# Gate and up products of a split-float32 feed-forward block: high and low x side by side in one 512-column matmul

## The reference

```python
def _rms_norm(x, g):
    y = x * lax.rsqrt(jnp.mean(x * x, axis=-1, keepdims=True) + NORM_EPS)
    return y * g

def _swiglu(x, w_gu, w_down):                  # d_ff 2816, eight times
    g, u = jnp.split(x @ w_gu, 2, axis=-1)
    return (jax.nn.silu(g) * u) @ w_down

def conv_ffn(x, w_up, conv_w, conv_b, w_down): # d_ff 3072, twice
    h = causal_depthwise_conv(x @ w_up, conv_w, conv_b)      # 3 taps along the tokens
    return (jax.nn.gelu(h[..., :D_FF_2]) * h[..., D_FF_2:]) @ w_down
```

## Time and profile before

| | us |
|---|---|
| median of 3 runs | 3186.62 |
| lowest, highest | 3185.95, 3188.76 |
| profiled execution, its own time | 3187.94 |
| its span in the trace | 3186.1 |
| PE busy | 2922.5 (92%) |
| DVE busy | 2079.8 (65%) |
| ACT busy | 1435.7 (45%) |
| mean granted TensorE clock, share of full speed | 0.957 |

### The profile page before, as it was taken

One profiled execution on the slowest core, in us unless ns is written; L12 is line 12 of the kernel. 1 busy time (PEld: TensorE's weight loads), 2 busy tenths in 40 slices (PEclk: granted clock), 3 DMA queues, 4 the chain that ended last, 5 costly groups with the idle time before them and its releaser, 6 DMA issues.

```text
span 3186.1 us, 46638 instructions
## 1 busy us (share of the span) xinstructions
PE 2922.5 (92%) x19567; PEld 2661.9 (84%) x19567; DVE 2079.8 (65%) x2681; ACT 1435.7 (45%) x1867; POOL 309.2 (10%) x391
## 2 busy tenths in 40 slices
PE   7997779999988999999799999877899889987898
PEld 7997769999975999995389999877899779885897
DVE  5668776565657656552665565787765767746776
ACT  4445435444444544442554444444444534444453
POOL 0005430000002000000000000345100000000000
PEclk9998889999999999999999999988999889997899
DMA  7553225676541665642146565432465446542553
GB/s 231 184 158 111 93 79 186 186 206 189 159 139 47 192 188 182 182 134 84 60 139 186 159 210 184 135 93 80 132 186 172 161 144 197 174 146 73 165 177 102
DMA packets 404053, 478.25 MB, mean 150 GB/s; under 512 B 16394, under 2 KB 331492, under 8 KB 403844
## 3 DMA queue, kind: packets, MB, share of 16 engines
q1 hardware_dynamic: 400432, 467.33, 47.0%
q0 software_dynamic: 1776, 6.77, 0.7%
q10 hardware_dynamic: 1636, 1.18, 0.1%
HBM read 474.17 MB, written 1.05 MB: 149 GB/s over the span
## 4 chain that ended last, share of the span: by engine, by line
PE 81%; DVE 14%; ACT 3%; issue 2%; ACTq 0%; DVEq 0%
PE Wk L570 15%; PE Wk L572 15%; PE Wk L571 15%; PE Y L570 9%; PE Y L571 9%; PE Y L572 9%; DVE w_lo L1511 3%; DVE work L1739 2%; PE Wk L578 2%; DVE work L1742 1%; PE Y L896 1%; PE Y L676 1%; PE Wk L869 1%; PE Y L804 1%; ACT w_hi L1103 1%
## 5 line engine op out<-in xcount | busy, mean ns | idle before, releaser
L1511 DVE TENSOR_TENSOR w_lo<-ring,w_hi 128x1024 fp32r<-128x1024 f32 x872 | 1061.0, 1242 | 628.8 <-ACT w_hi L1103 582.5
L570 PE MATMUL Wk<-xT_hi,w_hi 128*128 128x256 f32 x4320 | 1234.2, 286 | 19.3 <-DVE xT_lo L1543 15.9
L572 PE MATMUL Wk<-xT_hi,w_lo 128*128 128x256 f32 x4320 | 1227.9, 284 | 0.0
L571 PE MATMUL Wk<-xT_lo,w_hi 128*128 128x256 f32 x4320 | 1227.8, 284 | 0.0
L1103 ACT ACTIVATE w_hi<-ring 128x1024 fp32r<-128x1024 f32 x872 | 893.7, 1053 | 640.4 <-PE Wk L572 432.1
L570 PEld LDWEIGHTS Wk<-xT_hi,w_hi 128*128 128x128 f32 x4320 | 834.4, 193 | 27.0 <-issue 13.4
L571 PEld LDWEIGHTS Wk<-xT_lo,w_hi 128*128 128x128 f32 x4320 | 834.4, 193 | 4.7 <-issue 0.9
L572 PEld LDWEIGHTS Wk<-xT_hi,w_lo 128*128 128x128 f32 x4320 | 833.8, 193 | 0.0
L570 PE MATMUL Y<-w_hi,hid_hi 128*128 128x512 f32 x896 | 351.9, 393 | 4.3 <-DVE hid_lo L1597 4.3
L571 PE MATMUL Y<-w_lo,hid_hi 128*128 128x512 f32 x896 | 350.6, 391 | 0.0
L572 PE MATMUL Y<-w_hi,hid_lo 128*128 128x512 f32 x896 | 349.4, 390 | 0.0
(11 more groups left out here) (247 smaller groups left out, 3039.9 us busy)
## 6 DMA issues: line engine op xcount, KB each, us to landing
ring<-in_ffn_w_gu SPq DMA_DIRECT2D x352, 512.0 KB, 4.5
ring<-in_ffn_w_down SPq DMA_DIRECT2D x224, 512.0 KB, 4.4
ring<-in_ffn_w_up SPq DMA_DIRECT2D x96, 512.0 KB, 6.0
ring<-in_hg_w_in SPq DMA_DIRECT2D x80, 512.0 KB, 4.2
ring<-in_na_w_in SPq DMA_DIRECT2D x24, 512.0 KB, 4.5
ring<-in_hg_w_out SPq DMA_DIRECT2D x16, 512.0 KB, 4.1
ring<-in_lru_w_in SPq DMA_DIRECT2D x16, 512.0 KB, 4.5
ring<-in_kv_w SPq DMA_DIRECT2D x16, 512.0 KB, 4.9
```

Source lines behind the costliest of these rows:

```text
L570: pe.matmul(o, l_hi, r_hi, start=first, stop=False)
L571: pe.matmul(o, l_hi, r_lo, start=False, stop=False)
L572: return pe.matmul(o, l_lo, r_hi, start=False, stop=last)
L1511: dve.tensor_tensor(lo, raw(u), hi.bitcast(F32), ALU.subtract).then_inc(lo_done, 1)
```

## The change

The high and low parts of x lie side by side, `xT[:, k, 0, :]` and `xT[:, k, 1, :]`. For a block of weights, one matmul with the high weights runs over both (512 columns) and puts w_hi x_hi in the left half of a bank and w_hi x_lo in the right half; a second one with the low weights adds w_lo x_hi to the right half. So result and correction come apart, a product takes two banks (one for each f) and not one, and gate and up take all four banks of `Wk`: there is one set per chunk where there were two. ACT copies the right halves out (`save_rest`), DVE adds the left ones. PE waits before each gate product for the read of the last gate (`gate_read`, in cffn `conv_raw`), before each up product for that of the last up (`up_read`). In cffn ACT makes the tap with the bias. The products of the other sublayers keep their three matmuls.

```diff
-        xT_hi, xT_lo = sb("xT_hi", [P, KD, T], F32R), sb("xT_lo", [P, KD, T], F32R)
+        xT = sb("xT", [P, KD, 2, T], F32R)
+        xT_hi, xT_lo = xT[:, :, 0, :], xT[:, :, 1, :]
...
+        def with_rest(b):
+            return bank(b, 2).rearrange("p (f c t) -> p f c t", f=2, c=2)
...
+            def f_wide(u, b, f):
+                (t, h), (hi, lo) = u, split_of(u)
+                for i in range(4):
+                    k, c, o = 4 * h + i, 256 * i + P * f, bank(b + f)
+                    pe.matmul(o, hi[:, c:c + P], xT[:, k, :, :].rearrange("p c t -> p (c t)"), start=k == 0, stop=False)
+                    mm = pe.matmul(o[:, T:2 * T], lo[:, c:c + P], xT_hi[:, k, :], start=False, stop=k == KD - 1)
+                return mm
...
-                def gate_up(t, h):
-                    f_product(t, bank(2 * h))
-                    f_product(t + 1, bank(2 * h + 1))
+                def gate_up(j):
+                    if by_tokens(s):
+                        pe.wait_ge(conv_raw, 2 * (c0 + j) - 1)
+                    else:
+                        pe.wait_ge(gate_read, f0 + j)
+                    f_product(t0 + 3 * j - 1, 0, f_wide)
+                    if by_tokens(s):
+                        pe.wait_ge(conv_raw, 2 * (c0 + j))
+                    else:
+                        pe.wait_ge(up_read, f0 + j)
+                    f_product(t0 + 3 * j, 2, f_wide)
...
-                enter(s, (bank(0), bank(1)))
+                enter(s, (0, 2), f_wide)
...
                     if s == 0 and j == 1:
+                        pe.wait_ge(gate_read, 2)
                         first_parameters()
...
+            def save_rest(t, b, o):
+                act.wait_ge(unit_done, units_to(t))
+                act.activation(o, with_rest(b)[:, :, 1, :], ACT.Copy).then_inc(rest_saved, 1)
...
                     splits(g + 3)
+                    save_rest(g + 1, 0, gate_rest[:, j % 2])
                     if j == 0 and has_norm(s):
                         save_r(s)
                     splits(g + 4)
                     gate(j, j % 2, g)
+                    if j >= 2:
+                        act.wait_ge(hidden_ready, n0 + j - 1)
+                    save_rest(g + 2, 2, up_rest[:, j % 2])
                     rest(j, j % 2, g)
...
+                def last_tap(j, h, g):
+                    for gu in range(2):
+                        act.wait_ge(conv_raw, 2 * (c0 + j) + gu + 1)
+                        for f in range(2):
+                            act.activation(cf_out[:, h, gu, f, :], cf_raw[:, h, gu, f, 2:2 + T], ACT.Identity,
+                                           scale=..., bias=...).then_inc(conv_tap, 1)
...
                     dve.wait_ge(unit_done, units_to(g + 1))
-                    dve.tensor_tensor(wide(ff_silu[:, h, :]), wide(bank(2 * h)), r_wide(2), ALU.mult)\
+                    gate, up = with_rest(0), with_rest(2)
+                    dve.wait_ge(rest_saved, 2 * (n0 + j) + 1)
+                    dve.tensor_tensor(wide(ff_silu[:, h, :]), gate[:, :, 0, :], wide(ff_silu[:, h, :]), ALU.add)\
+                        .then_inc(gate_read, 1)
+                    dve.wait_ge(gate_read, f0 + j + 1)
+                    dve.tensor_tensor(wide(ff_silu[:, h, :]), wide(ff_silu[:, h, :]), r_wide(2), ALU.mult)\
                         .then_inc(gate_scaled, 1)
...
                     dve.wait_ge(unit_done, units_to(g + 2))
-                    hidden_parts(j, h, n0, ff_silu[:, h, :], bank(2 * h + 1))
+                    dve.wait_ge(rest_saved, 2 * (n0 + j) + 2)
+                    dve.tensor_tensor(wide(ff_hid[:, h, :]), up[:, :, 0, :], wide(ff_hid[:, h, :]), ALU.add)\
+                        .then_inc(up_read, 1)
+                    dve.wait_ge(up_read, f0 + j + 1)
+                    hidden_parts(j, h, n0, ff_silu[:, h, :], ff_hid[:, h, :])
...
-                    splits(g + 4)
-                    dve.wait_ge(conv_raw, 2 * (c0 + j + 1))
-                    for n, (gu, f) in enumerate(four):
-                        step(dve.tensor_scalar(cf_out[:, h, gu, f, :], cf_raw[:, h, gu, f, 2:2 + T], w(2, gu, f),
-                                               b(gu, f), ALU.mult, ALU.add), wait=n == 3)
+                    for gu in range(2):
+                        splits(g + 3 + gu)
+                        dve.wait_ge(unit_done, units_to(g + 1 + gu))
+                        dve.wait_ge(rest_saved, 2 * (n0 + j) + gu + 1)
+                        raw_ = cf_raw[:, h, gu, :, 2:2 + T]
+                        dve.tensor_tensor(raw_, with_rest(2 * gu)[:, :, 0, :], raw_, ALU.add).then_inc(conv_raw, 1)
+                    dve.wait_ge(conv_tap, 4 * (c0 + j + 1))
```

More of the change, by code:

```diff
@@ L208, in build @@
         y_part = sem("y_part")
+        gate_read, up_read, rest_saved = sem("gate_read"), sem("up_read"), sem("rest_saved")
         gate_scaled, z_read, c_mean, p_mean = sem("gate_scaled"), sem("z_read"), sem("c_mean"), sem("p_mean")
@@ L594, in f_product @@
                     for f in range(2):
-                        mm = f_part((t, h), o, f)
+                        mm = part((t, h), o, f)
                     mm.then_inc(unit_done, 1)
@@ L677, in turn, with enter @@
                 mm.then_inc(xT_psum, 1)
-            def enter(s, o):
+            def enter(s, o, part=f_part):
                 t = base[s]
@@ L685, in enter @@
                     pe.wait_ge(xT_ready, 4 * (s + 1))
-                    f_product(t, o[0])
-                    f_product(t + 1, o[1])
+                    f_product(t, o[0], part)
+                    f_product(t + 1, o[1], part)
                     return
@@ L704, in enter @@
                 for f in range(2):
-                    mm = f_part((t, 1), o[0], f)
+                    mm = part((t, 1), o[0], f)
                 mm.then_inc(unit_done, 1)
@@ L716, in enter @@
                 for f in range(2):
-                    mm = f_part((t + 1, 1), o[1], f)
+                    mm = part((t + 1, 1), o[1], f)
                 mm.then_inc(unit_done, 1)
@@ L1144, in save_r, with ffn_stages @@
                 act.activation(r_row[:, :], bank(6)[:, 0:T], ACT.Copy).then_inc(r_ready, 1)
-            def ffn_stages(s, chunks, gate, rest):
-                t0 = base[s]
+            def save_rest(t, b, o):
+                act.wait_ge(unit_done, units_to(t))
+                act.activation(o, with_rest(b)[:, :, 1, :], ACT.Copy).then_inc(rest_saved, 1)
+            def ffn_stages(s, chunks, gate_rest, up_rest, gate, rest):
+                t0, n0 = base[s], before(s, {"ffn": FF_CHUNKS, "cffn": CF_CHUNKS})
                 for j in range(chunks):
@@ L1193, in rest @@
                     hidden_hi(j, h, n0)
-                ffn_stages(s, CF_CHUNKS, both, rest)
+                ffn_stages(s, CF_CHUNKS, *(cf_raw[:, :, gu, :, 2:2 + T] for gu in range(2)), lambda j, h, g: None,
+                           last_tap)
             def sigmoid(z, done):
@@ L1492, in _ @@
                     act.preload_act_table_set("natural_log_exp_and_others")
-                if kind == "hg":
-                    hgrn(s, idx)
+                if kind in ("hg", "cffn"):
+                    {"hg": hgrn, "cffn": cffn}[kind](s, idx)
                 else:
-                    {"ffn": ffn, "cffn": cffn, "na": na, "mla": mla, "lru": lru, "stick": stick}[kind](s)
+                    {"ffn": ffn, "na": na, "mla": mla, "lru": lru, "stick": stick}[kind](s)
                 splits(end[s] + 1)
@@ L1610, in ffn @@
                     dve.wait_ge(unit_done, units_to(g + 1))
-                    dve.tensor_tensor(wide(ff_silu[:, h, :]), wide(bank(2 * h)), r_wide(2), ALU.mult)\
+                    gate, up = with_rest(0), with_rest(2)
[4 more added lines that the diff above has]
+                    dve.tensor_tensor(wide(ff_silu[:, h, :]), wide(ff_silu[:, h, :]), r_wide(2), ALU.mult)\
                         .then_inc(gate_scaled, 1)
+                    if s == 0 and j == 1:
+                        save_parameters(range(1, 7), 0)
                     splits(g + 4)
```

33 lines of the change are left out of this document (12 added, 21 removed).

## The result

The changed kernel takes 3212.4 us (median of 4 runs, 3210.6 to 3215.3), the kernel before, measured beside it, 3186.3 us (4 runs, 3185.8 to 3188.8). The ratio is 1.008, interval 1.0068 to 1.0093: 26 us or 0.8% **slower**. That is 21 us above the predicted time and at the upper edge of the range (3212), within rival (c)'s 3205 to 3214. Its profiled execution spans 3211.2 us, against 3186.1.

The account below looks back on a forecast made before the run. The prediction took TensorE (PE), busy 92% of the span, as the bound. Its terms, -42 + 25.6 + 8 + 0.7 + 12 = +4 us, gave about 3191 us beside the median of 3186.6, range 3174 to 3212.

Parts of the forecast that it names:

- rival (c): Slower: alternating widths cost wide matmuls their full 0.232 to 0.235 us, narrow ones no quicker; 3205 to 3214 us, chance 0.18.
- part 1: Gate and up products: three 256-column matmuls per weight block become one of 512 and one of 256, -42 us.
- chunk 1's gate waits: At each ffn's start PE waits for DVE's gate add, queued behind four w_lo: 8 x 3.2 = +25.6 us.
- ffn's end: In the last chunk an extra ACT copy and DVE add delay hid_lo, so PE waits: 8 x 1.0 = +8 us.
- cffn: The add and ACT's two up taps replace four DVE taps, about 0.3 us longer: +0.7 us for both sublayers.
- clock: Most of PE's eight waits at ffn starts are followed by a short stretch at clock 0.50: 8 x 1.5 = +12 us.
- all but the matmuls: The waits at ffn starts and ends, the cffn and the clock: 25.6 + 8 + 0.7 + 12 = 46.3 us.
- a sign of being wrong: For the alternating matmuls: the forecast is wrong if a pair takes over 0.352 or under 0.344 us.
- Rival (b): Faster: clock mostly stays up after the ffn-start waits and the matmul gain is at its upper end; 3174 to 3179, chance 0.16.
- Rival (d): The 13 ns belong to the columns, not the matmul, so a pair still costs 359.7 ns; 3233 us, chance 0.03.
- Rival (e): The eight ffn-start waits don't appear because DVE's four w_lo run ahead of r_row; 3154 us, chance 0.05.
- edit at nothing: At an ffn's start, chunk 1's up product comes 5.6 us behind its gate, so up_read is there first: no cost.

Follow-up runs that it names:

- e3: The changed kernel with each 512-column matmul made as two of 256 again, new banks and waits kept: 3234.6 us, ratio 1.0151.
- e5: The changed kernel, but at an ffn's start DVE makes the four w_lo, then adds the gate, and only then waits for r_row: 3173.5 us, ratio 0.9956.
- e6: On top of e5, each ffn's last up product made by three matmuls into one bank, without copy or add: 3164.7 us, ratio 0.9931.
- e4: The changed kernel, but at an ffn's start DVE adds the gate before making the four w_lo and waiting for r_row: 3190.8 us, ratio 1.001.
- e7: On top of e6, 200 of 224 products run all sixteen 512-column matmuls first, then all sixteen 256-column ones: 3148.0 us, ratio 0.9876.
- e1: The changed kernel with matmuls grouped, four of 512 columns and then four of 256: 3207.4 us, ratio 1.0064.
- e2: The changed kernel, but the narrow matmul adds to the left half of the bank instead of the right: 3211.8 us in one run.

## Why the prediction was right in its waits and wrong in its matmuls

| step | predicted | measured | from |
|---|---|---|---|
| matmuls (part 1) | -42 us, 348 ns a pair | -21 to -22 us, 352.8 ns | timeline; e3 |
| chunk 1's gate waits | 8 x 3.2 us | 8 x 3.2 us | timeline; e5 |
| ffn's end | 8 x 1.0 us | 7 x 1.06 and 1.34 us | timeline; e6 |
| cffn | +0.7 us | +1.1 us | timeline |
| clock | 8 x 1.5 us | 12.1 us; 7 of 8 fall | timeline, windows; e4 and e5 leave 9 and 13 |
| all but the matmuls | +46.3 us | +47.4 us | e3 |
| sum | +4 us | +26 us | runs |

**What failed is one term, the size of the gain in part 1.** It took 348 ns for a pair, "the value nearest to the alternating pattern", from two rows: one wide matmul behind a narrow one (0.24) and one narrow behind a wide one (0.11), together 0.35. Three things were wrong with that. First, each of those two is only the first matmul of a long run, and their sum 0.35 was already over the 348 that I took; I let the value slip towards that of undisturbed runs. Second, the rows show five disturbed wide matmuls in a row (0.232 on average), so that at a change in every matmul none would be free of it; I used that only for the far end of the range. Third, I gave each narrow one the full 0.11, and in the alternating stream only one in three is that quick. With 352.8 the pair fell even a little outside the bounds that I gave it (28 to 46.6 us; it is 24.9), and over the 0.352 us that I had named as a sign of being wrong. The down product's slower start, 4 us, I had not counted at all. So 17 of the 21 us are the pair and 4 the down product.

**Rival (c) is what happened**, by its own point of decision: a pair over 350 ns. Its rows spoke plainly for it, and 0.18 was too low a chance. Its picture was not exact either: the narrow one is somewhat quicker (116.5) and the wide one dearer (236.3) than it said. Rival (b) needed the clock to stay up behind more than five waits, and it did behind one. Rival (d) is out by e7: 359.7 - 347.1 = 12.6 ns go with every matmul that is saved, as long as widths aren't mixed. That is five times what the Trainium skill's 2.5 ns ("TensorE: Matmul & The Clock Gate", "Back-to-back issue gap") would give, a figure that the section states for a matmul by itself and not for a stream with weight loads. Rival (e) is out by the timeline.

**The waits were right** to a tenth of a microsecond, but for one, because they were read from the queue of the engine that must free the banks, not from its busy share. **The clock's total was right partly by luck**: eight falls of 1.5 us were forecast, and five of 1.3 to 1.4 and two of 2.7 us came, a number that differs from kernel to kernel (seven of eight in e1 and e3, six in e2). One edit at nothing held only under cover: "up_read is there first: nothing" is true behind a wait of 3.2 us and false without it, and e4 paid 1.6 us for it. The range's upper end, 3212, took in only the edge of (c), so the time lies there by rival (c) and not by the forecast.

What stays open is why a change of width costs what it does; the runs show how much and where, not the cause.

## What to carry to other kernels

Merging two matmuls into a wider one saves about 13 ns here for each matmul saved, but half of it is lost where widths then alternate (6.9 ns are left): run matmuls of one width together. Where one set of banks takes the place of two, list what stands in the reader's queue ahead of its first read at the start of a stage. That queue, not the reader's average load, is the price, and moving a wait that holds up work which doesn't need it took all of it back. And take a chain's last piece out of a new scheme if its extra steps lie on the path there.

## What the runs showed of the hardware

- A change of width between matmuls is felt over several of them. Behind a 256-column one, 512-column ones take 233, 236, 228, 232 and 231 ns, then 227; behind a 512-column one, 256-column ones take 113 or 114 and 119, then 120. It is the same in the kernel before, in e3 and in e7. Where widths alternate, wide ones take 233 to 241 without settling.
- Over their columns (213.3 and 106.7 ns at 2.4 GHz) both widths cost 13 ns at the full clock. At 0.50, 1.2 GHz, the distances in the changed kernel are 427 and 213 ns, the columns alone (426.7 and 213.3 ns): the extra doesn't show there.
- Silences of PE of one length, 3.1 to 3.2 us, at the starts of the ffn sublayers brought a low clock 27 times out of 32 (the changed kernel, e1, e2, e3), and the low stretches were 3.4 or 6.8 us long. They cost 1.3 to 1.4 and 2.7 us of time in the changed kernel. Behind the eight silences of 1.5 to 1.6 us in e4 the clock never fell.
- Whether the narrow matmul adds onto the left or the right half of what the wide one has just written made no difference (e2), and three narrow ones in a row onto the same columns cost 119.9 ns each (the kernel before).
